# Attention by pairs of heads in the second block: scores in two halves of the rows, fp32 values in two halves of the columns, a fused bias and minimum

## The reference, cut to what matters

```python
# even layer, for each of 8 heads (A_SCALE = 1/8)
s = q_h @ k_all.T * A_SCALE                  # 512 x 768, context queries 256 x 256
o = softmax(s) @ v_all
# odd layer, for each of 16 heads
kw, vw = kr[:, :, :, col_idx], vr[:, :, :, col_idx]    # windows of 16 columns
s_loc = einsum('bhqd,bhiqjd->bhqij', qr, kw) * C_SCALE + bias
s_ctx = einsum('bhqd,bhkd->bhqk', qr, kc_h) * C_SCALE
p = softmax(concatenate([s_loc, s_ctx]))
o = p_loc @ vw + p_ctx @ vc_h
```

## Time and profile before

| | |
|---|---|
| median of 3 runs | 4048.81 us (4045.4 to 4050.22) |
| the profiled execution | 4049.23 us |
| its span in the trace | 4047.4 us |
| mean granted clock of PE | 0.883 |
| PE busy | 3339.2 us, 83% of the span |
| PEld busy | 2692.7 us, 67% |
| DVE busy | 2663.4 us, 66% |
| ACT busy | 1920.7 us, 47% |
| POOL busy | 535.9 us, 13% |

### The profile page before, as it was taken

How to read it: one execution, slowest core, us unless ns; L and a number is a source line. 1 busy time by engine, 2 the same in 40 slices (tenths; PEclk the granted TensorE clock), 3 DMA queues, 4 the chain that set the end, 5 groups by cost and what they waited for, 6 DMA issues and landing times. The chain is left out here.

```text
span 4047.4 us, 48775 instructions
## 1 busy us (share of the span) xinstructions
PE 3339.2 (83%) x18076; PEld 2692.7 (67%) x18076; DVE 2663.4 (66%) x3072; ACT 1920.7 (47%) x2195; POOL 535.9 (13%) x395
## 2 busy tenths in 40 slices
PE   7386967969999956958877999993989877999994
PEld 6175834758888844716666888871766666888883
DVE  3744346469999944274457999985226647999983
ACT  2211214247777733004315777763214425777762
POOL 0020000002222200000001222211003201222210
PEclk9698977979999968967878999996988877999997
DMA  3701340269999934250136999976110046999993
GB/s 104 259 3 54 94 175 9 76 224 369 372 373 369 363 125 162 65 182 1 52 121 259 378 375 380 377 284 223 42 49 16 10 147 240 373 369 362 364 347 116
DMA packets 228239, 836.31 MB, mean 207 GB/s; under 512 B 70374, under 2 KB 93286, under 8 KB 147452
## 3 DMA queue, kind: packets, MB, share of 16 engines
q1 hardware_dynamic: 196268, 789.89, 53.2%
q0 software_dynamic: 31680, 43.92, 3.1%
q10 hardware_dynamic: 144, 0.52, 0.0%
HBM read 820.26 MB, written 85.43 MB: 224 GB/s over the span
## 5 line engine op out<-in xcount | busy, mean ns | idle before, releaser
L178 DVE TENSOR_TENSOR f3e_w_lo<-f_raw,f3e_w_hi 128x2048 fp32r<-128x2048 f32 x198 | 446.2, 2284 | 6.3 <-ACT f3e_w_hi L173 6.3
L178 DVE TENSOR_TENSOR f1e_w_lo<-f_raw,f1e_w_hi 128x2048 fp32r<-128x2048 f32 x192 | 432.8, 2284 | 6.1 <-ACT f1e_w_hi L173 6.1
L178 DVE TENSOR_TENSOR f2e_w_lo<-f_raw,f2e_w_hi 128x2048 fp32r<-128x2048 f32 x192 | 433.3, 2284 | 5.1 <-ACT f2e_w_hi L173 5.0
L173 ACT ACTIVATE f3e_w_hi<-f_raw 128x2048 fp32r<-128x2048 f32 x198 | 371.0, 1910 | 0.3 <-issue 0.3
L173 ACT ACTIVATE f1e_w_hi<-f_raw 128x2048 fp32r<-128x2048 f32 x192 | 360.0, 1910 | 0.0
L173 ACT ACTIVATE f2e_w_hi<-f_raw 128x2048 fp32r<-128x2048 f32 x192 | 359.6, 1908 | 0.0
L184 PE MATMUL l_psum_acc<-l_w_hi,m_hT_hi 128*128 128x512 f32 x288 | 115.9, 403 | 33.4 <-DVE l_w_lo L178 33.4
L178 DVE TENSOR_TENSOR l_w_lo<-l_raw,l_w_hi 128x512 fp32r<-128x512 f32 x70 | 48.3, 691 | 121.2 <-ACT l_w_hi L173 121.2
L185 PE MATMUL l_psum_acc<-l_w_lo,m_hT_hi 128*128 128x512 f32 x288 | 115.3, 400 | 0.0
L186 PE MATMUL l_psum_acc<-l_w_hi,m_hT_lo 128*128 128x512 f32 x288 | 115.3, 400 | 0.0
L184 PE MATMUL f3e_psum_gate<-f3e_w_hi,f3e_xT_hi 128*128 128x512 f32 x264 | 110.5, 419 | 3.3 <-DVE f3e_xT_lo L178 3.3
(11 more groups left out here) (817 smaller groups left out, 9514.0 us busy)
## 6 DMA issues: line engine op xcount, KB each, us to landing
f_raw<-in_moe_w_dram SPq DMA_DIRECT2D x390, 1024.0 KB, 7.5
f_raw<-in_w_gate_dram SPq DMA_DIRECT2D x64, 1024.0 KB, 8.2
f_raw<-in_w_up_dram SPq DMA_DIRECT2D x64, 1024.0 KB, 7.4
f_raw<-in_w_down_dram SPq DMA_DIRECT2D x64, 1024.0 KB, 6.9
ybuf<-m_zeros SPq DMA_DIRECT2D x11, 2048.0 KB, 18.8
h_adaw<-in_ada_w_dram SPq DMA_DIRECT2D x16, 1024.0 KB, 7.0
he_adaw<-in_ada_w_dram SPq DMA_DIRECT2D x16, 1024.0 KB, 6.5
l_raw<-in_w_in_dram SPq DMA_DIRECT2D x56, 256.0 KB, 2.7
```

The costliest lines, as they stand in the source:

```text
L173: return act.activation(dst, src, ACT.Copy)
L178: return v.tensor_tensor(dst, src, hi.bitcast(F32), ALU.subtract)
```

## The change

`attend_phase` is written anew, and `even_groups` and `odd_groups` become `even_pairs` and `odd_pairs`. The unit is a slot: both heads of a pair and one tile of 128 queries. ae has 16 slots with 768 keys and 8 with 256; ao has 32, in the order 0, 1, 3, 2 of the query tiles, so that the two middle tiles (384 near keys) and the two outer ones (256) alternate in part.

- Scores: the same three fp32r products, but the matmuls of the two heads alternate; head 0 has its operands in partitions 0 to 63, head 1 in 64 to 127. Each head has one score buffer of two banks, so that the scores of slot p wait for both exponentials of slot p - 1.
- Turned probabilities are copied as plain fp32, four tiles of head 0 and four of head 1 on ACT, the rest on DVE. There is no split of them.
- Values are plain fp32 matmuls, one for each key tile and head, with a stationary operand of 64 columns; head 0 writes partitions 0 to 63 of the result, head 1 64 to 127. They come two slots after the scores, in every slot. No halves of the values are made, neither on POOL in ao nor in e5.
- Row sums: DVE takes the reciprocals, POOL spreads them, PE turns them (two transposes for two slots) into the second half of the bank of the results. The result is normalised and split for two slots at a time; its low half is made on POOL.
- Bias in ao: the queries are scaled by -0.125 instead of 0.125, the mask has the opposite sign, and POOL subtracts the bias from it, so that the sums have the opposite sign. DVE takes a minimum over the 256 context columns and then, with one fused instruction, adds the masked bias to the near scores and takes the minimum of the sum and of the first minimum. The exponential gets a scale of -1. Each head has one buffer for the loaded bias; SP loads the next one when the second mask step of POOL (two of the seven) is done with it.
- The probabilities have tiles of their own, and the tiles of the row sums and of the result are 256 wide.

PE's part and order, in the new `attend_phase`:

```diff
+            def scores(p):
+                if p >= 1:
+                    pe.wait_ge(exp_done, 2 * p)
+                sl = slots[p]
+                for n, (lo, width, key) in enumerate(sl["parts"]):
+                    for z, (qz, kz) in enumerate(((0, 0), (0, 1), (1, 0))):
+                        for e in E:
+                            k = key(e)[kz]
+                            to = psS[:, 1024 * e + lo:1024 * e + lo + width]
+                            mm = pe.matmul(to, sl["q"][e][qz], k, start=(z == 0), stop=(z == 2))
...
+            def values(p):
+                for i in slots[p]["pieces"]:
+                    pe.wait_ge(ev_done[i], count[i][p])
+                if p >= 2 and p % 2 == 0:
+                    pe.wait_ge(norm_done, p // 2)
+                col = P * (slots[p]["col"] % 2)
+                n = slots[p]["nk"]
+                for k in range(n):
+                    for e in E:
+                        mm = pe.matmul(psO[HD * e:HD * e + HD, col:col + P], slots[p]["value"](k, e), tb[p % 2][:, e, k, :],
+                                       start=(k == 0), stop=(k == n - 1))
...
+            for p in range(NP + 3):
+                if p < NP:
+                    scores(p)
+                if has(p - 1, 1):
+                    turn(p - 1, 1)
+                if 0 <= p - 2 < NP:
+                    values(p - 2)
+                hf = half_at(p, 3)
+                if hf is not None:
+                    spread(hf)
+                if has(p - 1, 2):
+                    turn(p - 1, 2)
+                if has(p, 0):
+                    turn(p, 0)
```

ACT's loop, DVE's fused step and reciprocals, and the masks in POOL's loop, in this order:

```diff
+            for p in range(NP + 5):
+                hf = half_at(p, 4)
+                if hf is not None:
+                    act.wait_ge(b_done, hf + 1)
+                    act.activation(bs, psO[:, 256:512], ACT.Copy).then_inc(b_out, 1)
+                if has(p - 2, 1):
+                    evac(p - 2, 1)
+                if has(p - 1, 0):
+                    evac(p - 1, 0)
+                if p < NP:
+                    for e in E:
+                        exps(p, e)
+                if hf is not None:
+                    act.wait_ge(norm_done, hf + 1)
+                    d, src = slots[2 * hf]["result"](on)
+                    split_hi(act, d[0], src).then_inc(oh_done, 1)
...
+            def biased(p, e):
...
+                a = 1024 * e + start
+                v.wait_ge(c_done[e], p + 1)
+                link(v.tensor_reduce(cm[:, i:i + 1], psS[:, a:a + CTXL], AX.X, ALU.min))
+                v.wait_ge(s_done[e], p + 1)
+                if p % HEAD == 0:
+                    v.wait_ge(first_done[e], bias["parts"][0] * (u + 1))
+                elif p % HEAD == 2:
+                    v.wait_ge(second_done[e], bias["parts"][1] * (u + 1))
+                near = psS[:, a + CTXL:a + sl["n"]]
+                v.tensor_tensor_reduce(near, near, sl["add"](inner[u % 2][e], edge[e]), 1.0, cm[:, i:i + 1], ALU.add, ALU.min,
+                                       nm[:, i:i + 1]).then_inc(max_done, 1)
...
+                hf = half_at(p, 2)
+                if hf is not None:
+                    v.wait_ge(exp_done, 4 * hf + 4)
+                    mine = slice(4 * hf, 4 * hf + 4)
+                    v.reciprocal(rs[:, mine], sm[:, mine]).then_inc(rs_done, 1)
...
+                if bias and p + HEAD < NP:
+                    if p % HEAD == 1:
+                        masks(p // HEAD + 1, 0, first_done)
+                    elif p % HEAD == 3:
+                        masks(p // HEAD + 1, 1, second_done)
```

The copy stage and the scale of the queries:

```diff
-                    @block.scalar
-                    def _(act):
-                        for kv in range(2):
-                            split_hi(act, vp[0][:, :, P * kv + HD:P * kv + P], pj[:, :, 640 + HD * kv:704 + HD * kv]).then_inc(vh, 1)
...
-                        for d in vp:
-                            for z in range(3):
-                                v.memset(d[:, :, P * z:P * z + HD].bitcast(F32), 0.0).then_inc(dn, 1)
-                        for kv in range(2):
-                            cols = slice(P * kv + HD, P * kv + P)
-                            v.wait_ge(vh, kv + 1)
-                            split_lo(v, vp[1][:, :, cols], pj[:, :, 640 + HD * kv:704 + HD * kv], vp[0][:, :, cols]).then_inc(dn, 1)
...
-                      [(i, C, SEQ, both(qT, i, 0, SEQ), 0.125) for i in range(8)]
+                      [(i, C, SEQ, both(qT, i, 0, SEQ), -0.125) for i in range(8)]
```

More of the change, by code:

```diff
@@ L96, in constants @@
         j = 16 * t - 16 + np.arange(WIN)[None, :]
[L97 removed]
+        c[:, C_WIN + v * WIN:C_WIN + (v + 1) * WIN] = np.where((j >= start[:, None]) & (j < start[:, None] + 16), 0, -NEG)
     f = np.float32
@@ L734, in _, with attend_phase, half_at, has @@
                     jobs[i]["post"](v, link, psO[i % 2], rs[:, i:i + 1]).then_inc(post_done, 1)
[L737 to L775, removed]
+def attend_phase(nc, name, tab, slots, nk, start, prob, row, bias=None):
+    NP = len(slots)
+    E = range(2)
+    HEAD = 4
+    count = [[sum(1 for sl in slots[:p + 1] if i in sl["pieces"]) for p in range(NP)] for i in range(3)]
+    def half_at(p, lag):
+        hf, r = divmod(p - lag, 2)
+        return hf if r == 0 and 0 <= hf < NP // 2 else None
+    def has(p, i):
+        return 0 <= p < NP and i in slots[p]["pieces"]
     with Scope(nc, name) as s:
@@ L802, in _ @@
             def _(sp):
[L803 to L837, removed]
@@ L839, in _ @@
         @block.tensor
         def _(pe):
[L841 to L889, removed]
@@ new lines, in turn @@
+            def turn(p, i):
+                es, k0, k1 = slots[p]["pieces"][i]
+                pe.wait_ge(exp_done, 2 * p + es[-1] + 1)
+                if count[i][p] > 1:
+                    pe.wait_ge(ev_done[i], count[i][p] - 1)
+                j = 0
+                for e in es:
+                    for k in range(k0, k1):
+                        mm = pe.transpose(ring[i][:, j * P:(j + 1) * P], prob[2 * (p % 2) + e][:, k * P:(k + 1) * P],
+                                          tab[:, C_IDENT:C_IDENT + P])
+                        j += 1
+                mm.then_inc(t_done[i], 1)
@@ new lines, in evac, with exps @@
+            def evac(p, i):
+                act.wait_ge(t_done[i], count[i][p])
+                if p >= 2:
+                    act.wait_ge(pv_done, p - 1)
+                act.activation(turned_to(p, i), turned_from(p, i), ACT.Copy).then_inc(ev_done[i], 1)
+            def exps(p, e):
+                sl = slots[p]
+                i = 2 * p + e
+                act.wait_ge(max_done, i + 1)
+                if p >= 2:
+                    for n in sl["pieces"]:
+                        if count[n][p - 2]:
+                            act.wait_ge(t_done[n], count[n][p - 2])
+                act.activation(prob[2 * (p % 2) + e][:, 0:sl["n"]], psS[:, 1024 * e + start:1024 * e + start + sl["n"]], ACT.Exp,
+                               scale=-1.0 if bias else 1.0, bias=nm[:, i:i + 1], accum_out=sm[:, i:i + 1]).then_inc(exp_done, 1)
@@ new lines, in even_pairs, with part, result @@
+def even_pairs(qT, kT, values, oT):
+    slots = []
+    for rows, n in ((range(XT0, NTA), NTA * P), (range(XT0), CTXL)):
+        nk = n // P
+        for m in range(4):
+            for t in rows:
+                def part(lo, w, m=m):
+                    return lo, w, lambda e: [h[HD * e:HD * e + HD, m // 2, lo:lo + w] for h in kT]
+                def result(on, m=m, lo=t * P):
+                    return [d[:, m, lo:lo + 256] for d in oT], on
+                slots.append(dict(q=[[d[HD * e:HD * e + HD, m, t * P:(t + 1) * P] for d in qT] for e in range(2)],
+                                  parts=[part(lo, min(512, n - lo)) for lo in range(0, n, 512)], n=n, nk=nk, col=len(slots),
+                                  pieces={0: ((0,), 0, 4), 1: ((1,), 0, 4), 2: ((0, 1), 4, 6)} if nk == NTA else {1: ((0, 1), 0, 2)},
+                                  result=result,
+                                  value=lambda k, e, m=m: values(k, m // 2)))
+    return slots
```

325 lines of the change are left out of this document (125 added, 200 removed).

## The result

| | before | after |
|---|---|---|
| median | 4047.11 us (4 runs, 4039.61 to 4050.22) | 3890.43 us (4 runs, 3883.69 to 3891.05) |
| profiled execution | 4049.23 | 3890.40 |
| span | 4047.4 | 3888.3 |
| PE / DVE / ACT busy | 3339.2 / 2663.4 / 1920.7 | 3197.4 / 2558.4 / 1901.4 |

The ratio is 0.9612, with a 95% interval of 0.9594 to 0.9629: 157 us less, where 3905 (144 under the profiled 4049) was forecast and 3865 to 3985 was the range. In the traces the even attention (ae) went from 158.5 to 98.5 us, the odd one (ao) from 234.3 to 141.7, and the copy stage with what follows it lost 3.3. The other phases together moved by about 3 us, as they do between two executions of one kernel (f1e, the first block's expert phase, lasts 591.6 or 594.9 us in runs that don't touch it).

A forecast was written before the change was run, and what follows sets the result against it. PE was taken to bound both attention phases, partly at 1.2 GHz. Savings of 55 us in ae, 89 in ao and 3 in the copy stage, 147 in all, took 4049 to 3902, stated as 3905; range 3865 to 3985.

The forecast's parts named there:

- PE's unit costs and the overlap of the halves: PE in both attentions: 0.23 us per 512-column product, 0.12 per 256, 0.11 per value record; the two heads' matmuls overlap fully.
- Rival A: Score and value matmuls in both attentions: neither row nor column halves overlap, some 85 us more, 3990; chance 0.12.
- Changes between 64 and 128 rows or columns: PE's mode changes between scores, transposes and values: 0.2 us each, four in an even slot, 0.8 us.
- The even slot: Slot of ae: PE's sum 4.6 us, just over a 4.4 loop through DVE and ACT; 4.7 taken, context slots 2.4.
- The odd slot: Slot of ao: PE 3.7 us, loop 3.7, ACT 3.5; 4.0 taken for chains waiting on each other, bounds 3.6 and 4.9.
- The fused operation: DVE's add-minimum in ao: one pass, the plain add (0.42 or 0.56 us) plus 0.1 for the accumulator.
- Rival B: DVE's fused operation in ao costs two passes: odd slots 4.9 us, 27 us more, 3932; chance 0.12.
- Bias loads: SP's loads and POOL's masks in ao: about 13 us in four slots of 16 us, hidden with 3 us to spare.
- The start of ao: First slots of ao: second head's loads, masks, add and exp aren't hidden; slot 1's scores start near 3032, 12 us in.
- Clock: PE's clock in both attentions: value matmuls from slot 2 bring full clock from about 1846 (ae) and 3041 (ao), no dips.
- rival C: Clock dips as before once in four slots as PE waits in the loop: twelve times 3.4 us, 40 us, 3945; chance 0.12.
- D: Rival: the clock never rises in either attention, as waiting for both exps leaves PE short of work: 4079, slower; chance 0.04.

## Why the prediction was right, point by point

- **PE's unit costs and the overlap of the halves** (0.23, 0.12 and 0.109 for a pair): right. Rival A falls. Its price of 85 us stays untested: with the heads one after the other the two attentions were 45 us longer, but even then PE started the second head's matmuls early, so the halves overlapped in part.
- **Changes between 64 and 128 rows or columns**: put at 0.2 us each. The slot of 4.31 holds 1.04 + 1.31 + 1.31 of matmuls, so four changes took 0.65, 0.16 each.
- **The even slot**: 4.7 forecast, 4.42 measured. PE's sum of 4.6 was some 0.16 too high by the changes of mode, and the 0.1 for imperfect fit wasn't needed. The loop through the exponentials was put at 4.4 and is 4.27. The context slots were 2.4, as forecast, save the first two (3.19 and 2.97, which still hold values of slots with 768 keys).
- **The odd slot**: 4.0 forecast, 3.67 measured. The sum of the loop, 3.7, was right (the slots with 384 near columns take 3.95, the others 3.39); the 0.3 on top for three chains that wait for each other was the mis-sized term, some 9 us over 28 slots. That loop and not PE sets ao: with two of the four or five key tiles left in PE's values its slots stayed. The Trainium skill's sentence in TensorEngine Tiling (Array Packing), Performance Considerations, that packing doesn't speed up the evacuation of PSUM, describes this slot; the trace agrees (PE busy 120.7 of 141.7 us, at no loss when it had less to do).
- **The fused operation**: 0.49 and 0.63, between the plain add and the add plus 0.1. Rival B falls. The Trainium skill's Vector Engine (DVE) Microarchitecture Reference, section 7, puts the halved rate of a scalar-tensor-tensor operation on two SBUF sources; here one source is in PSUM, and these rows show no halving (0.63 us for 384 columns, against 0.56 for the plain add).
- **Bias loads, "hidden, with 3 us to spare"**: this step failed. The low half queued behind the masks was named, and POOL waiting for DMA while DVE waits for POOL was the sign that the prediction gave for being wrong. The chain was put at 9.4 us of loads, 1.9 for five masks and 1.5 for four more, 13 in all. From 2978.63, the second mask step, to the end of the next five masks at 2991.87 it was 13.24, where the forecast's 9.4 and 1.9 and the 0.8 of the two masks that free the buffer make 12.1; the late landing of one load (1.4) explains the difference. And the slots are 3.67 us, so four give 14.7 and not 16, the low half and the copy of the reciprocals add 1.1 to POOL's round, and the first rounds begin late: the second mask step of the second pair of heads ran at 2978.63, 1.5 us after the scores of its slot 3 had begun (2977.10), where in a later round it comes 1.6 us before them (3009.59 against 3011.18). The long step makes up for that delay. It cost 5.7 us with the two small ones, which two buffers took away.
- **The start of ao**: slot 1 at +12 forecast, +12.35 measured.
- **Clock**: no dips forecast; there was one in ao, after the wait for the loads, and none in ae, so rival C (twelve dips) and D fall. In ao full clock came 20.8 us after its start, 1 us after the first value matmul; 21 was forecast (3041). In ae the reason for the rise was wrong. I had it wait for value matmuls and put it at about 1846, 15 us into ae; it came at 1832.4, 9.9 us in, and the first value matmul of ae started at 1835.01. In the stretch just before (1829.00 to 1832.40) PE was busy for 3.23 us, most of it with transposes over all 128 rows. In the traces of all nine kernels since the change the clock rose 8.0 to 12.2 us after the start of ae, each time before the first value matmul (12.5 to 14.1 us in). Which part of PE's work lifts the clock stays open. Full clock from slot 2 on saved some 3 us against the sum, 1 of it because slots 0 and 1 took 5.38 and 5.24 us: their forecast of 5.8 is 0.35 more than the terms given for it make.
- **What the clock is worth**: the traces show 1.2 GHz for 129 us of the two attentions before and for 30 after. Had PE set the pace in all of it, full clock would have halved these times; so at most some 50 of the 157 us are the clock's, an estimate from these two numbers. No run separates it from the shorter work of PE.
- **Copy stage**: 3 us forecast, 3.3 measured.

So the sum missed by 4 us in ae's slots, 3 at its start and 9 in ao's slots on one side, and by the 5.7 of the loads and 3 in the first steps and tails on the other. Together that is 7 or 8 of the 15 us between 3905 and 3890; most of the rest is in phases that the change doesn't touch, and the rounding up of the sum from 3902.

## What to carry to other kernels

In this kernel two heads with 64 channels in the two halves of PE's rows (0.23 us for a pair of 512 columns), and with 64 output columns in the two halves of its columns (0.109 us for a pair of 128), cost what one costs, if their matmuls alternate. Once PE is that fast, price the loop between the engines by its longest chain and take that sum as it is; then look at what was hidden behind the old, slower pace, as loads with a single buffer here, and give it the pace of the new slot, from its first round on, and leave room for one load that lands 1.4 us late. Where a phase opens with a wait for loads and the phase before leaves the DMA queue idle, issue them there.

## What the runs showed of the hardware

In these traces matmuls that use the other half of the array start ahead of earlier ones in the program: with six score matmuls of one head and then six of the other, the seventh started within 0.01 us of the third (both at 1882.51); with twelve value records and then twelve, the thirteenth started within 0.01 us of the ninth. From the first start to the last it was 1.6 us for the scores, where all in turn would be 2.1, and 2.2 for the values, where 24 records of 0.109 would be 2.5. The accumulator read of the fused operation on DVE (0.14 us) overlaps the next instruction: both start at 2986.27.
